# The far rows of a key and value cache, loaded by stretch of 16 and then by position

## What is computed

```python
DIL_GROUPS = ((128, 1), (512, 4), (2048, 16))
def dilated_sample(q, k_all, v_all, rel_bias, window, dil, wbuf):
    T = q.shape[1]
    n = window // dil
    steps = jnp.arange(n + 1)
    idx = wbuf + jnp.arange(T)[:, None] - steps[None, :] * dil
    ...
    kg, vg = k_all[:, idx], v_all[:, idx]
    bias = rel_bias[t5_bucket(steps * dil)].T.astype(jnp.float32)
    s = jnp.einsum('bthd,btmhd->bhtm', q, kg) * ATTN_SCALE + bias[:, None, :]
    p, lse = masked_softmax_stats(s, valid[None, None])
    o = jnp.einsum('bhtm,btmhd->bthd', p, vg)
```

## Time and profile before

| | |
|---|---|
| time, median of 3 runs | 1910.31 us (1908.27 to 1917.51) |
| time of the profiled execution | 1916.21 us |
| its span, first to last instruction | 1914.6 us |
| TensorE busy | 1729.9 us, 90% |
| VectorE, ScalarE busy | 861.6 us, 708.3 us |
| mean granted TensorE clock | 0.938 of full speed |
| bytes moved | 373.32 MB, 195 GB/s over the span |
| the cache attention | about 639 to 855 us of the span |
| transfers of far rows | 16 of keys and 16 of values, 256 KB each |
| transfers of newer rows | 16 of keys and 16 of values, 1024 KB each |

### The profile page before, as it was taken

The page is one execution under the profiler, slowest core; times in us unless marked ns, Lnnn a source line. Parts: engine busy times, 40 slices in busy tenths (PEclk is TensorE's granted clock), DMA queues, the critical chain, the costliest instruction groups (busy, mean ns, idle before and its releaser), DMA issues.

```text
span 1914.6 us, 30013 instructions
## 1 busy us (share of the span) xinstructions
PE 1729.9 (90%) x12190; PEld 1514.9 (79%) x12190; DVE 861.6 (45%) x1425; ACT 708.3 (37%) x980; POOL 76.8 (4%) x134
## 2 busy tenths in 40 slices
PE   6779999999999756667997999999999999999997
PEld 2338888888888523326887999999999999999997
DVE  1234344345556322225337444445454446565663
ACT  1213244335446221124324333334243334554552
POOL 2000000001111000000000000000000000000000
PEclk9869899899999878778998999999999999999999
DMA  9997586667776587666774545444554454555551
GB/s 325 304 343 239 171 278 220 196 205 239 242 237 212 150 228 215 199 179 202 259 242 135 172 140 173 144 161 148 166 165 132 160 177 154 172 164 174 171 164 43
DMA packets 283749, 373.32 MB, mean 195 GB/s; under 512 B 7601, under 2 KB 208659, under 8 KB 283193
## 3 DMA queue, kind: packets, MB, share of 16 engines
q1 hardware_dynamic: 275920, 350.93, 56.8%
q0 software_dynamic: 7680, 20.36, 3.2%
q10 hardware_dynamic: 18, 0.07, 0.0%
HBM read 361.45 MB, written 11.97 MB: 195 GB/s over the span
## 4 chain that ended last, share of the span: by engine, by line
PE 78%; SPq 7%; DMA 6%; DVE 3%; issue 2%; ACT 2%; DVEq 0%; POOL 0%; ACTq 0%; POOLq 0%
PE ps L772 22%; PE ps L773 21%; PE ps L774 21%; PE ps L719 4%; SPq L520 4%; DMA ring<-in_w_ada 4%; SPq L521 3%; DMA vals<-in_cache_v_win 2%; PE ps L853 1%; PE ps L726 1%; PE ps L899 1%; DVE wlo L1525 1%; PE ps L711 1%; PE ps L692 1%; PE ps L1035 1%
## 5 line engine op out<-in xcount | busy, mean ns | idle before, releaser
L772 PE MATMUL ps<-hhi,whi 128*128 128x288 f32 x3136 | 948.0, 302 | 21.5 <-DVE wlo L1525 15.4
L773 PE MATMUL ps<-hlo,whi 128*128 128x288 f32 x3136 | 934.1, 298 | 0.0
L774 PE MATMUL ps<-hhi,wlo 128*128 128x288 f32 x3136 | 933.7, 298 | 0.0
L772 PEld LDWEIGHTS ps<-hhi,whi 128*128 128x128 f32 x3136 | 598.2, 191 | 61.4 <-issue 51.2
L773 PEld LDWEIGHTS ps<-hlo,whi 128*128 128x128 f32 x3136 | 598.0, 191 | 0.8
L774 PEld LDWEIGHTS ps<-hhi,wlo 128*128 128x128 f32 x3136 | 597.7, 191 | 0.0
L1518 DVE TENSOR_TENSOR wlo<-ring,whi 128x1024 fp32r<-128x1024 f32 x178 | 210.1, 1220 | 86.2 <-ACT whi L1184 85.0
L1184 ACT ACTIVATE whi<-ring 128x1024 fp32r<-128x1024 f32 x178 | 184.2, 1056 | 171.3 <-PE ps L774 163.3
L1525 DVE TENSOR_TENSOR wlo<-ring,whi 128x1024 fp32r<-128x1024 f32 x128 | 155.3, 1221 | 159.7 <-ACT whi L1192 159.1
L1192 ACT ACTIVATE whi<-ring 128x1024 fp32r<-128x1024 f32 x128 | 132.6, 1050 | 121.9 <-PE ps L774 109.3
L719 PE MATMUL ps<-ring,c 128*32 128x512 f32 x768 | 119.5, 702 | 34.6 <-DMA ring<-in_w_ada 34.1
(11 more groups left out here) (265 smaller groups left out, 1173.8 us busy)
## 6 DMA issues: line engine op xcount, KB each, us to landing
ring<-in_w_ada SPq DMA_DIRECT2D x96, 1024.0 KB, 5.4
ring<-in_w_up SPq DMA_DIRECT2D x88, 1024.0 KB, 5.1
ring<-in_w_in SPq DMA_DIRECT2D x48, 1024.0 KB, 5.8
ring<-in_w_down SPq DMA_DIRECT2D x32, 1408.0 KB, 6.7
ring<-in_cache_k_win SPq DMA_DIRECT2D x16, 1024.0 KB, 15.6
vals<-in_cache_v_win SPq DMA_DIRECT2D x16, 1024.0 KB
ring<-in_w_out SPq DMA_DIRECT2D x16, 1024.0 KB, 7.2
ring<-in_state_gla POOLq DMA_DIRECT2D x8, 512.0 KB, 7.2
```

The lines of the kernel that those rows point to most:

```text
L772: mm(out, w_hi, x_hi, start=start, stop=False)
L773: mm(out, w_hi, x_lo, start=False, stop=False)
L774: return mm(out, w_lo, x_hi, start=False, stop=stop)
```

## The change

The far rows of a stretch of 16 positions now lie next to one another on the partitions. Partition r held position 16 * (r % 32) + r // 32 (all first positions of the 32 stretches, then all second ones, and so on); it now holds 16 * (r // 4) + r % 4. The source of the transfer has the dimensions (32 stretches, 4 positions, 512 columns) where it had (4 positions, 32 stretches, 512 columns). The tables on the host are made in the same order (`TS` is 4).

```diff
     r = np.arange(P)
-    far = 16 * (r % 32) + r // 32
+    far = 16 * (r // TS) + r % TS
     pos = np.concatenate([far, PAST // 2 + np.arange(PAST // 2)])
...
-                far = rows[0:PAST // 2, cols].rearrange("(a r) c -> r a c", r=16)[0:TS]
+                far = rows[0:PAST // 2, cols].rearrange("(a r) c -> a r c", r=16)[:, 0:TS]
                 sp.dma_start(view[:, 0, :], far).then_inc(landed[0], 16)
```

## The result

The changed kernel takes 1827.98 us, the median of 4 runs (1825.34 to 1832.47); the kernel before takes 1909.45 in the same series. The ratio is 0.957, with a 95% interval of 0.954 to 0.960.

What follows compares the result with a forecast made beforehand. Four DMA engines carrying the far rows were taken to bound the cache stage; pairs falling from 6.15 to 4.2 us, followed through buffer waits, gain 57.8 us from the 1910.31 us median: forecast 1852 us, range 1837 to 1868.

Steps and rivals of the forecast that it cites:

- eight engines: Rival: the far rows go to only eight engines, 4.9 us a pair, gain 38, 1872 us; chance 0.05.
- a conflict in the memory: Rival: sixteen engines stepping alike through the cache disturb each other, a pair 5.9 us, 1899 us; chance 0.04.
- no effect: Rival: the far transfer in its new form is still carried by four engines, 1910 us; chance 0.04.
- a loss: Rival: far rows read by stretch take longer on sixteen engines, 5.2 us at 50 GB/s, about 1993 us; chance 0.03.
- The price of a pair: Cache stage, far plus recent rows after the change: 3.4 + 0.15 + 0.66 to 0.85 us, taken as 4.2 us.
- The far rows' end of the bound: Far rows on 16 engines, each keeping 24.8 GB/s: 396 GB/s, 0.66 us a pair.
- the 0.15 us that it kept: Left over between the 6.05 us worked out for an old pair and the 6.15 to 6.23 measured.
- The other end: Low end of a pair's time, at the weight stream's 374 GB/s with a full queue: 3.5 us, 1841 us.
- TensorE's turn: TensorE's time for eight pairs in the cache stage: 30.25 us busy plus 1.5 us of waits, 31.8 us.
- TensorE becomes the bound: Rival: pairs come at the weight stream's rate, a DMA turn falls under TensorE's 31.8 us, 1841 us; chance 0.10.
- The schedule: Cache stage followed through landings and buffer waits: last values land at 785.5 us instead of 843.27, gain 57.8 us.
- the two silences of the DMA: Sign: the DMA engines run empty for a short while near 658 and near 763 us, while loads wait for buffers.

Runs made afterwards that it cites:

- dense4: Changed kernel with the far transfer's outer dimension back at 4, reading 4 blocks of 32 successive rows (other rows than the reference's); 1914.60 us.
- dense8: Changed kernel with the far transfer's outer dimension at 8, reading 8 blocks of 16 successive rows (other rows than the reference's); 1878.36 us.
- far_once: Changed kernel with far rows loaded for the first group alone, later groups using them again (other rows than the reference's); 1829.36 us.
- the second trace: The kernel before, profiled once more without an edit; 1905.95 us in one run.

## Why the prediction was too cautious

**What bounded the kernel: right.** Four engines carried the far rows; dense4 puts that bound back by the outer dimension alone, and the low level of the share goes to 0.54 with 8 and vanishes with 32.

**Sixteen engines after the change: right.** The share has no lower level left. The rivals of eight engines, of a conflict in the memory, of no effect and of a loss did not come; what eight engines would have cost is in dense8, 1878 us against the 1872 worked out.

**The price of a pair: the step that failed.** "I take 4.2 us, since the rows of the same transfers in the same stage are nearer than those of the weights." A pair takes 3.39 us (1.311 MB at 386 GB/s). The far rows' end of the bound was good: each engine keeps the 24 GB/s that the four had alone. The newer rows' 3.4 us was the wrong term: their 304 to 313 GB/s was no property of theirs but part of what the change removes. By themselves they move at 389 GB/s (far_once, 657 to 675 us), 1.049 MB in 2.7 us. Counted by the busiest engine, the pair went from 128 KB (a quarter of the far rows and a sixteenth of the newer ones) to 80 KB; at 24.2 GB/s that is 5.4 and 3.39 us. The new pair agrees with its 3.39. The old one took 6.15, so about 0.75 us of it was slowness of the engines while all worked: from 656 to 659 us a packet took 108 ns on the mean, in the changed kernel it takes 85. The prediction carried this slowness over: of the 0.8 us by which its pair was too long, 0.7 is the newer rows' term, the rest the 0.15 us that it kept. The runs by block show that sixteen engines that write into a part of the partitions drop to 217 GB/s with nobody idle. That it is the same clash that slowed the stage before, where each of four engines wrote a block of 32 partitions while all sixteen wrote newer rows, fits (264 GB/s with all at work) but is argued: four engines that write only where nobody else does were not tried. The other end, 3.5 us from the weight stream, was close but a little high as well. Its windows are no bad luck of that execution: the second trace has 341 and 342 GB/s in them, where the first had 342 and 374. What that stream can do shows earlier, at 25 to 50 us, with 392 GB/s in the second trace and only 335 in the first.

**TensorE's turn: mis-sized too.** It was put at 31.8 us from a window in which TensorE stood waiting for values and came back at the lower level of its clock. Without those waits the clock stays at the higher level (1.00 from 651 to 731 us) and the turn is 28.1 us. The rival "TensorE becomes the bound", given 0.10, is what happened, at a better price than worked out.

**The schedule: right.** The same steps with 3.4 and 28.1 us give: fifth pair issued at 658.8, landed at 666.3; the first group's values at 683.3, read 5.6 us later (the measured time from the first value product to the next load is 5.7 to 5.9); two turns, 745.1; last values 4.1 + 13.6 us after, 762.8 us. Measured, put on the axis of the first trace (10.0 us later), 763.6. With the right pair and TensorE's old figures (7.7 us to read the values, a turn of 31.8) they give 772.3: so of the 21.9 us that the forecast of 785.5 missed, 13.2 are the pair's and 9.5 TensorE's, less 0.8. The pair alone would have moved the forecast to 1839 us, still inside the range; it took both. The first keys' landing, the two silences of the DMA (the second one 20 us earlier than forecast, like all late steps) and the hidden weights of the output projection came as described: the first split of these weights starts 31.4 us after the last values, against 30.9 before. TensorE is busy all through both silences (3.00 of 3 us in each window), and at the end it waits 1.48 us for the last values.

## What to carry to other kernels

In these runs the outer dimension of a transfer's source decided how many DMA engines carry it (4, 8, and all sixteen for 32): a mean DMA share that sits on a fraction like 4/16 for a while, with the issuing queue blocked, is the sign. Look on the target's side as well: each large transfer should by itself spread over all 128 partitions. Four in a row that cover them together, a block of 32 each, ran at 217 GB/s. And a rate that was measured beside the fault is not the rate after its repair, neither of the transfers next to it nor of an engine that lost its clock in waiting; take both from a stretch without the fault, and from more than one execution.

## What the runs showed of the hardware

All 16 engines together held 386 GB/s for 80 us, in pieces of 2 KB, 24 GB/s each. Transfers to 32 and to 64 neighbouring partitions ran at 217 and 210 GB/s with every engine shown as busy, a packet taking 144 ns to 32 of them; to 32 partitions four apart it took 87, to all 128 it took 81. An issue to every fourth partition took 0.74 to 0.79 us of SyncE, against 0.50 for a transfer of the same size to all partitions. The same weight stream at the start (25 to 50 us) ran at 335 to 343 GB/s in five of the twelve traces, at 371 or 372 in three and at 391 or 392 in four; between the two traces of the kernel before, 335 and 392, the start of the cache stage moved by 10 us.
